# Three-block transformer kernel: the two MLPs' up products with chained weight and input sums, and a new order where each MLP begins

## The chip, the cores and the metric

One core of a Trainium2 chip runs the whole program, one launch. The metric is the time of that launch on the device in microseconds (us), smaller is better. Most of the program is float32 matrix products done on TensorE (PE) as three products of split operands: every operand is cut into a rounded high part (written by ScalarE, ACT) and the remainder, the low part (written by VectorE, DVE, for inputs and by GpSimd, POOL, for weights), and high x high, high x low and low x high are accumulated. SyncE (SP) issues all DMA transfers.

## What is computed

Three blocks follow one another on a sequence of 1024 tokens with 1024 channels: a convolution and a gated recurrence with a mixer, then a block with chunked attention, and then one with an mLSTM. The second and the third block end in an MLP, and the change is in these two (here MLP 2 and MLP 3):

```
hdn = jnp.square(jax.nn.relu(hdn))                       # hdn = rms_norm(x) @ w_up, 1024 x 4096
x = x + jnp.einsum('bsf,fd->bsd', hdn, w_down[l])        # second block
x = layer_norm_3(ALPHA * x + squared_relu_mlp(x, w_ff1[l], w_ff2[l]), ln2_g[l], ln2_b[l])   # third block
```

## The kernel before

Activations stand transposed: 128 channels on the partitions, tokens along the row, so that X is eight tiles of 128x1024. An MLP has 32 tiles of 128 hidden channels. The program treats them in two ways.

**First ups.** The first four tiles (u = 0 to 3) are plain products. The tokens come in two halves (hf 0 and 1, 512 tokens), so there are eight half products, here called h0 to h7. `gemm_half` (L701) is one: eight k tiles, three matmuls of 512 columns each, 24 matmuls. Its weights are one slab of 128x1024: SP fetches it into raw (two places), ACT copies it to wh (L1513, place i % 2), POOL writes wl in two halves (L3662). ACT's split of slab i waits until slab i-2 has been used, since wh has two places. Before the change h0 to h7 use eight slabs, base+0 to base+7: the four weights are loaded and split once for each token half. After each half product ACT evacuates with relu (L2044), DVE squares it (L3041), and SP stores it.

**Fast ups.** The other 28 tiles are 14 pairs. A pair's 2x2 block product (hidden 2, inputs 2x512 channels, tokens 2x512) is done with seven products instead of eight (`fast_mlp`, L1206): 98 products of 12 matmuls, in three groups of four (high x high, high x low, low x high; L1226). The weights of a product are 128x512 in a ring of four places; ACT makes the high part (`w_high`, L2068, runs at L2081) once the product four before is done, POOL the low part (L3679). Of the seven weights of a pair two are blocks of the matrix as it is, and five are sums that DVE makes (`w_add`, L3057, runs at L3071). The inputs are seven as well: two are plain, five are sums of X blocks, made once per MLP: for each of four k tiles a sum by DVE (L3051), a high part by ACT (L2050) and a low part by DVE (L3054). The seven results go to eight PSUM banks in turn; DVE combines them (`hidden`, L3083, adds at L3089), then relu and square in one (L3121, L3130), then five sums that the down products need, and SP stores all (`keep_pair`). A bank is free for the product eight later when its last reader is done (`up_free`, L572).

**Fast downs.** 7 passes of 14 products (L1245), again 12 matmuls each. Weights and hidden tiles come in by DMA; ACT makes the high part of the hidden tile (L2086), DVE the low part (`act_low`, L3073, runs at L3075). DVE's turn n of its loop also makes the weight sum for product n+5, and its in-order queue puts `act_low` of m+3 behind that sum. SP reloads X from DRAM (B<-keep_x) for the later additions.

The order on each engine is the order in which the functions are written. Nothing is scheduled by a planner.

Of the kernel before, what the change touches and what calls it, by code (L numbers as in the profile page):

```python
# [19 lines left out]
KT = 8  # L20
META = 16
# [37 lines left out]
GATES3, POOL3, OUT3, MLP3 = 154, 175, 179, 191  # L59
NSLAB = 206  # L60


def twice(a, b):
# [5 lines left out]
WEIGHTS = [*range(92), *twice(92, 96), *twice(96, 100), *range(100, 122), *twice(122, 126), *twice(126, 130),  # L69
           *twice(130, 134), *twice(134, 138), *range(138, 159), *twice(159, 163), *twice(163, 167), 167,  # L70
           *twice(168, 171)]
# [4 lines left out]
def down_at(base, j, hf=0):  # L76
    return base + 8 + j + hf * (4 - HALVED[base])
# [11 lines left out]

PAIRS = 14  # L90
NUP, NFAST = 7 * PAIRS, 14 * PAIRS
UP_ORDER = (2, 4, 5, 3, 1, 7, 6)
# [11 lines left out]
TAKEN = {4: "21", 3: "12", 1: "22+", 7: "11++", 6: "22++"}  # L104
# [3 lines left out]
def fast_product(n):  # L108
    return UP_ORDER[n % 7] if n < NUP else DOWN_ORDER[(n - NUP) // PAIRS]


SUMMED = [n for n in range(NFAST) if fast_product(n) in W_SUM]
# [161 lines left out]
def program(nc, A, tables, draft):  # L274
# [159 lines left out]
    def spent(i):  # L434
        return c.gemm(i, 1 if i in DOWN else 0)
# [41 lines left out]
    def up_half(u, hf):  # L477
        n = (4 * hf + u) % 6
        return side_of(ub[:, n // 2, :], n % 2)
# [68 lines left out]
    def act_slot(z, m):  # L548
        return IN[2][z][:, m % 4, :]
# [29 lines left out]
    def slab_behind(i):  # L579
        return next((m for m in (MLP2, MLP3) if i in (m + 8, m + 9)), None)  # L580
# [3730 lines left out]
```

## Time and profile before

| | us |
|---|---|
| median of 3 runs (3541.1 to 3544.37) | 3543.8 |
| the profiled execution | 3541.67 |
| its span | 3540.4 |
| TensorE busy, of the span | 3437.9 (97%) |
| VectorE / GpSimd / ScalarE busy | 2406.9 / 1414.0 / 1323.4 |
| granted TensorE clock, mean | 0.99 |

MLP 2's first ups, fast ups and fast downs lie at about 1754 to 1809, 1811 to 2093 and 2093 to 2369 us of the span, MLP 3's at about 2833 to 2896, 2897 to 3181 and 3181 to 3458. TensorE hardly ever waits, so what matters are the few gaps in its stream: their sum, who ends each, and the stretches in which its granted clock is half.

### The profile page before, as it was taken

The numbers are of one execution on the slowest core, as the hardware profiler recorded it, in microseconds if no ns is written. First come the engines' busy times: TensorE is split into PE (matmuls) and PEld (weight loads), VectorE is DVE, ScalarE is ACT, GpSimd is POOL, SyncE is SP. The second block draws the span as 40 slices with busy tenths as digits, with TensorE's granted clock in tenths as the row PEclk, the third lists the DMA queues.
The fourth block names the chain that finished last, engine by engine and source line by source line (L and its number), as shares of the span: only waits on it lengthen the run. The fifth ranks groups of instructions, "written<-read, shape, count | busy, mean of one in ns | idle before, by whom it ended". The sixth has DMA issues, their size and how long they took to land.

```text
span 3540.4 us, 46507 instructions
## 1 busy us (share of the span) xinstructions
PE 3437.9 (97%) x17822; PEld 2839.0 (80%) x17822; DVE 2406.9 (68%) x3137; ACT 1323.4 (37%) x1950; POOL 1414.0 (40%) x916
## 2 busy tenths in 40 slices
PE   8999999999999999999979999999999979999997
PEld 7998888889888887887868877887777758887886
DVE  6677608999653474345488878777566668887786
ACT  5565522222231343443332234444322342234443
POOL 4444422232233451112465545445113455554443
PEclk9999999999999999999999999999999989999998
DMA  3111021111242341111434357544012243447552
GB/s 110 37 31 37 31 90 42 60 60 59 85 143 95 106 153 38 32 32 42 161 110 150 145 213 236 172 122 134 30 36 82 62 135 145 147 159 274 158 172 78
DMA packets 147532, 372.22 MB, mean 105 GB/s; under 512 B 16368, under 2 KB 16624, under 8 KB 147312
## 3 DMA queue, kind: packets, MB, share of 16 engines
q1 hardware_dynamic: 147312, 369.24, 31.1%
q8 instruction: 143, 2.34, 0.3%
q14 instruction: 77, 0.63, 0.1%
HBM read 280.05 MB, written 89.13 MB: 104 GB/s over the span
## 4 chain that ended last, share of the span: by engine, by line
PE 86%; DVE 7%; ACT 2%; DMA 2%; issue 2%; POOL 1%; SPq 0%; DVEq 0%; ACTq 0%
PE psum L669 48%; PE psum L1226 15%; PE psum L1245 14%; PE psum L825 1%; PE psum L1123 1%; PE psum L1090 1%; PE psum L1105 1%; POOL wl L3662 1%; DMA raw<-in_wdn 1%; PE psum L770 1%; POOL wl L3679 0%; DMA B<-keep_x 0%; PE psum L850 0%; PE psum L849 0%; DVE k L3362 0%
## 5 line engine op out<-in xcount | busy, mean ns | idle before, releaser
L3662 POOL TENSOR_TENSOR wl<-raw,wh 128x512 fp32r<-128x512 f32 x412 | 612.4, 1508 | 1316.5 <-ACT wh L1513 1316.5
L669 PE MATMUL psum<-hh,wh 128*128 128x512 f32 (+2 forms) x2864 | 920.7, 389 | 35.5 <-POOL wl L3662 31.2
L669 PE MATMUL psum<-hh,wl 128*128 128x512 f32 (+2 forms) x2864 | 881.5, 376 | 0.0
L669 PE MATMUL psum<-hl,wh 128*128 128x512 f32 (+2 forms) x2864 | 878.0, 375 | 0.0
L669 PEld LDWEIGHTS psum<-hh,wh 128*128 128x128 f32 x2864 | 510.7, 189 | 142.0 <-issue 54.1
L669 PEld LDWEIGHTS psum<-hl,wh 128*128 128x128 f32 x2864 | 526.4, 189 | 93.2
L669 PEld LDWEIGHTS psum<-hh,wl 128*128 128x128 f32 x2864 | 527.2, 189 | 86.5
L3679 POOL TENSOR_TENSOR wl<-wsum,wh 128x512 fp32r<-128x512 f32 x280 | 421.9, 1515 | 391.4 <-ACT wh L2081 391.4
L2081 ACT ACTIVATE wh<-wsum 128x512 fp32r<-128x512 f32 x280 | 176.7, 634 | 484.4 <-PE psum L1245 207.6
L1513 ACT ACTIVATE wh<-raw 128x1024 fp32r<-128x1024 f32 x206 | 217.3, 1055 | 271.7 <-PE psum L669 244.9
L2612 DVE SCALAR_TENSOR_TENSOR psum<-av,vec,psum 128x1024 f32<-128x1024 f32 x232 | 299.2, 1290 | 7.9
L1245 PE MATMUL psum<-hh,wh 128*128 128x512 f32 x784 | 215.2, 396 | 7.8 <-DVE hl L3075 4.0
L1245 PE MATMUL psum<-hl,wh 128*128 128x512 f32 x784 | 212.9, 393 | 0.0
L1245 PE MATMUL psum<-hh,wl 128*128 128x512 f32 x784 | 212.6, 393 | 0.0
L1245 PEld LDWEIGHTS psum<-hh,wh 128*128 128x128 f32 x784 | 147.4, 188 | 43.4 <-issue 4.8
L1245 PEld LDWEIGHTS psum<-hl,wh 128*128 128x128 f32 x784 | 147.7, 188 | 34.2
L1245 PEld LDWEIGHTS psum<-hh,wl 128*128 128x128 f32 x784 | 147.4, 188 | 33.9
L1226 PE MATMUL psum<-hx,wh 128*128 128x512 f32 x672 | 169.5, 394 | 0.0
L3710 POOL TENSOR_TENSOR work<-fb 128x1024 f32<-128x1024 f32 x48 | 115.9, 2423 | 122.4 <-PE psum L825 96.9
L3075 DVE TENSOR_TENSOR hl<-hh_f,hh 128x512 fp32r<-128x512 f32 x100 | 118.1, 1181 | 54.9 <-ACT hh L2086 54.8
L1226 PEld LDWEIGHTS psum<-hx,wh 128*128 128x128 f32 x672 | 126.1, 188 | 29.6
L3075 DVE TENSOR_TENSOR hl<-hl_f,hh 128x512 fp32r<-128x512 f32 x96 | 114.6, 1195 | 46.4 <-ACT hh L2086 46.4
(517 smaller groups left out, 5070.7 us busy)
## 6 DMA issues: line engine op xcount, KB each, us to landing
raw<-in_wts SPq DMA_DIRECT2D x206, 512.0 KB, 3.6
keep_hidden<-B SPq DMA_DIRECT2D x168, 256.0 KB, 2.1
hh_f<-keep_hidden SPq DMA_DIRECT2D x100, 256.0 KB, 2.8
hl_f<-keep_hidden SPq DMA_DIRECT2D x96, 256.0 KB, 2.8
raw<-in_wup SPq DMA_DIRECT2D x28, 512.0 KB, 4.4
rawx<-in_wup SPq DMA_DIRECT2D x28, 512.0 KB, 4.3
raw<-in_wdn SPq DMA_DIRECT2D x56, 256.0 KB, 3.3
rawx<-in_wdn SPq DMA_DIRECT2D x56, 256.0 KB, 3.4
```

Source lines behind the costliest of these rows:

```text
L669: ins = pe.matmul(out, w, x[:, k, c0:c0 + width], start=first and n == only[0], stop=final and n == only[-1])
L770: ins = pe.matmul(x[:, n * 128:(n + 1) * 128], rr[:, slot, a:a + 1].to_broadcast([P, P]), ident, start=True, stop=True)
L825: ins = pe.matmul(x[s0:s0 + 64, a + t0:a + t0 + 64], left[:, b + s0:b + s0 + 64], right[:, b + t0:b + t0 + 64], start=True, stop=True)
L1226: ins = pe.matmul(x, w[:, k * 128:(k + 1) * 128], y[:, k, :], start=(w is a and y is xh and k == 0), stop=(w is b and k == 3))
L1245: ins = pe.matmul(down_bank(base, pi, j), w[:, j * 128:(j + 1) * 128], y, start=(t == 0 and w is a and y is xh), stop=(t == PAIRS - 1 and ...
L1513: se.activation(wh[:, s, :], raw[:, s, :], COPY).then_inc(*c.hi.tick(i))
L2081: se.activation(w_ring(wh, base, n), w_src(base, n), COPY).then_inc(*c.w_hi.tick(base, n))
L2612: ve.scalar_tensor_tensor(Cb[:, m, :] if last else taps, u[:, j:j + T], V("conv_w", 8 * j + m), taps, MUL, ADD).then_inc(*c.cv_dve.tick(*( ...
L3075: ve.tensor_tensor(act_slot(1, m), act_raw(m), fp(act_slot(0, m)), SUB).then_inc(*c.a_lo.tick(base, m))
L3662: gp.tensor_tensor(wl[:, s, a], raw[:, s, a], fp(wh[:, s, a]), SUB).then_inc(*c.lo.tick(i, p))
L3679: gp.tensor_tensor(w_ring(wl, base, n), w_src(base, n), fp(w_ring(wh, base, n)), SUB).then_inc(*c.w_lo.tick(base, n))
L3710: gp.tensor_tensor(lev(lv).rearrange("p (n b) -> p n b", b=2 * hs), bv, bv[:, :, hs - 1:hs].to_broadcast([P, T // (2 * hs), 2 * hs]), SUB) ...
```

## The change

The arithmetic that TensorE does is the same in count: 8 half products and 98 + 98 fast products in each MLP. Around them:

- **Slabs.** The half products run in the order `FIRST_UPS`: tiles 0, 1, 2, 3 on the first token half, then 2, 3, 1, 0 on the second. Tiles 2 and 3 keep their slabs (`HELD`) for both, so an MLP's first ups need six slabs (base+0 to base+5), not eight.
- **Squares.** ACT squares what it evacuated, right behind the relu and waiting for it; DVE no longer does.
- **Fast ups in another form.** Seven products still, but three weights are plain and four are sums, chained (a sum is made of another sum); the inputs are three plain and four sums, chained. The sums to combine the results are seven adds by DVE and one ACT copy a pair, where they were eight and two; each add waits for the one ahead of it.
- **Order.** The products of pairs 0 and 1 are interleaved at the start: (0,1) (1,1) (0,2) (1,2) (0,3) ..., so that the first four need no weight sum and the first five no input sum. Pair 0's weight blocks go to rawx and are fetched before the first ups' last slabs. DVE's input sums have explicit waits for POOL's low parts (`lo(base + 4, 1)`, `lo(base + 5, 1)`, `w_lo(base, 1)`).
- **Up to down.** DVE's last hidden sums are spread over the first six down products, SP stores them between the down loads, and X comes back in halves from down product 12 on, not in whole tiles from 6 on. The first down weights wait for up product 94 (fourth from last), because the cache lies on another input.
- **MLP 3.** The offsets that ACT adds to X (`offset`) are done in halves, the first halves between the relus.

```diff
-UP_ORDER = (2, 4, 5, 3, 1, 7, 6)
+FIRST_UPS = ((0, 0, 0), (1, 1, 0), (2, 2, 0), (3, 3, 0), (2, 2, 1), (3, 3, 1), (4, 1, 1), (5, 0, 1))
+HELD = (2, 3)
+UP_ORDER = (1, 3, 2, 7, 6, 5, 4)
+UPS = ((0, 1), (1, 1), (0, 2), (1, 2), (0, 3), (0, 7), (0, 6), (0, 5), (0, 4), (1, 3), (1, 7), (1, 6), (1, 5), (1, 4),
+       *((j, p) for j in range(2, PAIRS) for p in UP_ORDER))
+UP_ALONE = {1: (0, 0), 2: (0, 1), 4: (1, 1)}
+UP_SUM = {5: ((1, 0), ADD, (1, 1)), 6: (5, SUB, (0, 0)), 3: ((0, 1), SUB, 6), 7: ((0, 0), SUB, (1, 0))}
+UP_IN = {7: ((1, 1), SUB, (0, 1)), 6: (7, ADD, (0, 0)), 5: ((0, 1), SUB, (0, 0)), 4: ((1, 0), SUB, 6)}
+SUM_TURN = {**{5: (1, (5,)), 6: (1, (6, 3)), 7: (1, (7,))},
+            **{7 * j + z: (j + 1, ps) for j in range(1, PAIRS - 1) for z, ps in ((3, (5,)), (4, (6, 3)), (5, (7,)))}}
-TAKEN = {4: "21", 3: "12", 1: "22+", 7: "11++", 6: "22++"}
+TAKEN = {2: "11", 6: "u1", 5: "u3", 7: "u2", 3: "12", 4: "21"}
...
+        def relu_half(base, q):
+            i, u, hf = FIRST_UPS[q]
+            e = int(hf and i in HELD)
+            se.wait_ge(*c.gemm(base + i, e))
...
+            x = up_half(q)
+            se.activation(x, pairs.of(base + i, e)[:, hf, :], ACT.Relu).then_inc(*c.ev.tick("up", base, u, hf))
+            se.wait_ge(*c.ev("up", base, u, hf))
+            se.activation(x, x, SQUARE).then_inc(*c.ev.tick("squared", base, u, hf))
...
+            in_highs(base, 7)
+            for q in range(4, 8):
+                if q < 6:
+                    se.wait_ge(*c.gemm(base + FIRST_UPS[q][0], 1))
+                    split(base + q)
+                relu_half(base, q)
+                if q < 6:
+                    in_highs(base, (6, 5)[q - 4])
...
         def hidden(base, n):
...
+            if p == 2:
...
+                add(h[0, 0], h[1, 0], at[2], "11")
+            elif p == 6:
+                add(h[1, 0], h[1, 0], at[6], "u1")
+            elif p == 5:
+                add(h[0, 1], h[1, 0], at[5], "u3")
...
+                add(h[1, 1], h[0, 1], at[7], "22")
+                add(h[1, 0], h[1, 0], at[7], "u2")
+                add(h[0, 1], h[0, 1], at[3], "12")
+                row_done(base, j, 0)
             else:
+                add(h[1, 0], h[1, 0], at[4], "21")
+                if j < PAIRS - 1:
+                    row_done(base, j, 1)
...
         def fast_mlp(base):
-            for u in range(4):
-                squared(base, u, 0)
-            for u, p in enumerate((4, 1, 7)):
-                in_sums(base, p)
-                squared(base, u, 1)
...
+            in_sums(base, 7)
+            in_sums(base, 6)
+            in_lows(base, 7)
+            ve.wait_ge(*c.lo(base + 4, 1))
+            in_sums(base, 5)
+            in_lows(base, 5)
+            for p in UP_SUM:
+                up_weights(base, 0, p)
+            ve.wait_ge(*c.lo(base + 5, 1))
+            ve.wait_ge(*c.gemm(base + 5, 0))
+            in_sums(base, 4)
+            in_lows(base, 6)
+            ve.wait_ge(*c.w_lo(base, 1))
+            in_lows(base, 4)
...
             if p == 3:
-                sp.wait_ge(*c.fast(base, NUP - 6 if t < 8 else NUP - 5))
+                sp.wait_ge(*c.fast(base, NUP - 4 if t < 8 else NUP - 1))
...
-            for m in range(6):
-                down_step(base, m)
-            keep_pair(base, PAIRS - 1)
+            last = {5: (2,), 6: (5,), 7: (6,), 8: (3,), 9: (1,), 10: (4,), 11: (7,)}
```

**Where MLP 2's first ups end, on ACT.** ub<-psum is the relu of a half product, wh<-raw 128x1024 the split of a slab, hx and hh the high parts of input sums, wh 128x512 that of a fast product's weight. Before:

```order
L1513 ACTIVATE wh<-raw 128x1024 [waits product_done,weight_in0]
L2044 ACTIVATE ub<-psum 128x512 [waits product_done]
L2050 ACTIVATE hx<-hx_f 128x512 [waits input_sum] x4
L1513 ACTIVATE wh<-raw 128x1024 [waits product_done,weight_in1]
L2044 ACTIVATE ub<-psum 128x512 [waits store2,product_done]
L2050 ACTIVATE hx<-hx_f 128x512 [waits input_sum] x4
L2044 ACTIVATE ub<-psum 128x512 [waits store3,product_done]
L2081 ACTIVATE wh<-wsum 128x512 [waits product_done,weight_sum]
L2081 ACTIVATE wh<-raw 128x512 [waits product_done,block1,block0]
L2050 ACTIVATE hh<-hl_f 128x512 [waits input_sum] x4
```

Now (L2068 is the square):

```order
L1532 ACTIVATE wh<-raw 128x1024 [waits product_done,weight_in1]
L2066 ACTIVATE ub<-psum 128x512 [waits product_done]
L2068 ACTIVATE ub<-ub 128x512 [waits evacuated_act]
L2073 ACTIVATE hx<-hx_f 128x512 [waits input_sum] x4
L2066 ACTIVATE ub<-psum 128x512 [waits store2,product_done]
L2068 ACTIVATE ub<-ub 128x512 [waits evacuated_act]
L2066 ACTIVATE ub<-psum 128x512 [waits store3,product_done]
L2068 ACTIVATE ub<-ub 128x512 [waits evacuated_act]
L2108 ACTIVATE wh<-rawx 128x512 [waits product_done,block0]
L2108 ACTIVATE wh<-raw 128x512 [waits product_done,block2]
L2108 ACTIVATE wh<-rawx 128x512 [waits product_done,block0]
```

The square stands between the last relu and the first product's weight, which is a plain block and no sum, and no input sums stand between the first four weights.

**The same place on DVE.** hx_f and hl_f are input sums, hx and hl their low parts, wsum a weight sum. Before:

```order
L3041 TENSOR_TENSOR ub<-ub 128x512 [waits evacuated_act]
L3051 TENSOR_TENSOR hx_f<-B 128x512 x4
L3054 TENSOR_TENSOR hx<-hx_f,hx 128x512 [waits input_sum_hi] x4
L3041 TENSOR_TENSOR ub<-ub 128x512 [waits evacuated_act]
L3051 TENSOR_TENSOR hx_f<-B 128x512 x4
L3054 TENSOR_TENSOR hx<-hx_f,hx 128x512 [waits input_sum_hi] x4
L3041 TENSOR_TENSOR ub<-ub 128x512 [waits evacuated_act]
L3071 TENSOR_TENSOR wsum<-raw 128x512 [waits block1,block0]
L3041 TENSOR_TENSOR ub<-ub 128x512 [waits evacuated_act]
L3071 TENSOR_TENSOR wsum<-raw 128x512 [waits block1,block0] x2
L3051 TENSOR_TENSOR hl_f<-B 128x512 x4
```

Now:

```order
L3067 TENSOR_TENSOR hx_f<-B 128x512 [waits normed] x4
L3067 TENSOR_TENSOR hx_f<-hx_f,B 128x512 [waits normed,input_sum] x4
L3073 TENSOR_TENSOR hx<-hx_f,hx 128x512 [waits input_sum_hi] x4
L3067 TENSOR_TENSOR hx_f<-B 128x512 [waits normed,weight_lo]
L3067 TENSOR_TENSOR hx_f<-B 128x512 [waits normed] x3
L3073 TENSOR_TENSOR hx<-hx_f,hx 128x512 [waits input_sum_hi] x4
L3088 TENSOR_TENSOR wsum<-rawx 128x512 [waits block1,block0]
L3088 TENSOR_TENSOR wsum<-wsum,rawx 128x512 [waits weight_sum]
L3088 TENSOR_TENSOR wsum<-rawx,wsum 128x512 [waits weight_sum]
L3088 TENSOR_TENSOR wsum<-rawx 128x512
L3067 TENSOR_TENSOR hl_f<-B,hx_f 128x512 [waits normed,input_sum,product_done,weight_lo]
```

The four first sums stand ahead of the rest, the squares are gone, and there are waits for weight_lo (POOL's part of slabs base+4 and base+5) and for product_done, the end of h7.

**Where MLP 2's ups turn into downs, on DVE.** The adds read PSUM, the 128x1024 instruction is relu and square of a row, hl<-hh_f,hh is the low part of a down product's hidden tile. Before:

```order
L3089 TENSOR_TENSOR B<-psum,B 128x512 [waits fast_copied]
L3089 TENSOR_TENSOR B<-psum,B 128x512 [waits fast_products]
L3089 TENSOR_TENSOR B<-psum,B 128x512 [waits fast_dve]
L3089 TENSOR_TENSOR B<-psum,B 128x512
L3075 TENSOR_TENSOR hl<-hh_f,hh 128x512 [waits hidden_hi]
L3089 TENSOR_TENSOR B<-B,psum 128x512 [waits fast_dve,fast_products]
L3089 TENSOR_TENSOR B<-B,psum 128x512 [waits fast_dve]
L3075 TENSOR_TENSOR hl<-hh_f,hh 128x512 [waits hidden_hi]
L3089 TENSOR_TENSOR B<-B,psum 128x512 [waits fast_dve,fast_products]
L3121 SCALAR_TENSOR_TENSOR B<-B 128x1024 [waits fast_dve]
L3089 TENSOR_TENSOR B<-B 128x512 [waits hidden_out6,fast_dve]
L3075 TENSOR_TENSOR hl<-hh_f,hh 128x512 [waits hidden_hi]
```

Now:

```order
L3103 TENSOR_TENSOR hl<-hh_f,hh 128x512 [waits hidden_hi]
L3142 TENSOR_TENSOR B<-B,psum 128x512 [waits fast_products]
L3103 TENSOR_TENSOR hl<-hh_f,hh 128x512 [waits hidden_hi,fast_dve]
L3142 TENSOR_TENSOR B<-B,psum 128x512 [waits fast_products]
L3142 TENSOR_TENSOR B<-B,psum 128x512 [waits hidden_out6,fast_dve]
L3142 TENSOR_TENSOR B<-B,psum 128x512 [waits fast_dve] x2
L3113 SCALAR_TENSOR_TENSOR B<-B 128x1024 [waits fast_dve]
L3103 TENSOR_TENSOR hl<-hh_f,hh 128x512 [waits hidden_hi,fast_dve]
L3142 TENSOR_TENSOR B<-B,psum 128x512 [waits fast_products]
L3103 TENSOR_TENSOR hl<-hh_f,hh 128x512 [waits hidden_hi,fast_dve]
L3113 SCALAR_TENSOR_TENSOR B<-B 128x1024
```

Up product 92's bank, the first that a down product writes, is given free by the last add of the group that stands behind product 96 (the row with x2); before, it was given free by the adds behind product 94.

## Rows read from the trace of the kernel before

**Rows 1.** The page, busy time of an engine.

```profile
PE 3437.9 (97%) x17822; PEld 2839.0 (80%) x17822; DVE 2406.9 (68%) x3137; ACT 1323.4 (37%) x1950; POOL 1414.0 (40%) x916
```

**Rows 2.** Waits of PE, whole span: us in total, times, longest.

```profile
PE psum L669 <- POOL wl L3662: 31.2, 8, 11.5
PE psum L1226 <- POOL wl L3679: 12.5, 2, 6.2
PE psum L1226 <- ACT wh L2081: 5.2, 4, 1.3
PE psum L1245 <- DVE hl L3075: 4.0, 2, 2.0
PE psum L1245 <- ACT wh L2081: 3.8, 2, 1.9
```

**Rows 3.** Windows: length, busy and count of PE, PEld, DVE, ACT, POOL, clock, DMA.

```profile
1776.00:1836.00 60.00, 42.05 (x164) 32.46 (x163) 46.59 (x61) 23.92 (x39) 37.70 (x17) 0.89 0.35 113
1900.00:2000.00 100.00, 100.00 (x433) 80.92 (x432) 89.05 (x103) 28.02 (x47) 53.58 (x37) 1.00 0.41 149
2816.00:2836.00 20.00, 15.63 (x66) 12.43 (x64) 17.03 (x22) 9.48 (x14) 10.26 (x8) 0.91 0.18 54
2857.00:2923.00 66.00, 43.70 (x163) 33.50 (x162) 43.05 (x61) 28.78 (x45) 38.28 (x18) 0.84 0.49 167
2093.00:2135.00 42.00, 38.10 (x164) 30.45 (x163) 23.94 (x23) 15.97 (x27) 19.44 (x14) 1.00 0.89 333
3180.00:3227.00 47.00, 43.08 (x179) 34.33 (x178) 28.76 (x29) 18.40 (x31) 20.15 (x16) 0.96 0.91 343
```

**Rows 4.** Windows of a few us behind gaps of PE.

```profile
1798.60:1805.40 6.80, 3.37 (x8) 2.72 (x9) 2.17 (x4) 0.00 (x0) 4.51 (x2) 0.50 0.21 36
3218.60:3222.00 3.40, 3.40 (x8) 2.67 (x9) 3.30 (x4) 1.51 (x3) 2.11 (x2) 0.51 1.05 396
```

**Rows 5.** Timeline of ACT: start, duration, instruction, idle time before; MLP 2's slab base+5.

```profile
1780.26 1.06 ACT L1513 ACTIVATE wh<-raw 128x1024 fp32r<-128x1024 f32 x1 [3.67 <-DMA raw<-in_wts]
```

**Rows 6.** Timeline of POOL, MLP 2's first ups and first fast products.

```profile
1781.41 3.37 POOL L3662 TENSOR_TENSOR wl<-raw,wh 128x512 fp32r<-128x512 f32 x2 [2.43 <-ACT wh L1513]
...
1794.03 9.09 POOL L3662 TENSOR_TENSOR wl<-raw,wh 128x512 fp32r<-128x512 f32 x2 [5.25 <-ACT wh L1513]
...
1817.82 8.29 POOL L3679 TENSOR_TENSOR wl<-wsum,wh 128x512 fp32r<-128x512 f32 x1 [4.21 <-ACT wh L2081]
```

**Rows 7.** Timeline of DVE, one run of input sums in MLP 2's first ups.

```profile
1795.27 2.48 DVE L3051 TENSOR_TENSOR hx_f<-B 128x512 f32<-128x512 f32 x4
```

**Rows 8.** Timeline of ACT: last relu, first weight; a dependent pair; MLP 3's offsets.

```profile
1809.43 0.60 ACT L2044 ACTIVATE ub<-psum 128x512 f32<-128x512 f32 x1 [11.01 <-PE psum L669]
1809.92 0.62 ACT L2081 ACTIVATE wh<-wsum 128x512 fp32r<-128x512 f32 x1
...
2825.80 0.71 ACT L2316 ACTIVATE B<-B,vec 128x512 f32<-128x512 f32 x1
2826.53 0.63 ACT L2318 ACTIVATE hh<-B 128x512 fp32r<-128x512 f32 x1
...
2863.50 5.29 ACT L2328 ACTIVATE B<-B,vec 128x1024 f32<-128x1024 f32 x5
```

**Rows 9.** Timelines: ACT's first down weight; DVE's adds in a pair, an act_low.

```profile
2086.08 0.63 ACT L2081 ACTIVATE wh<-hx_f 128x512 fp32r<-128x512 f32 x1 [1.60 <-DMA hx_f<-in_wdn]
...
1928.56 2.61 DVE L3089 TENSOR_TENSOR B<-psum,B 128x512 f32<-128x512 f32 x4 [0.58 <-ACT B L2104]
...
2094.60 1.78 DVE L3075 TENSOR_TENSOR hl<-hh_f,hh 128x512 fp32r<-128x512 f32 x1
```

**Rows 10.** DMA issues (KB each, median us to landing); DVE's wait, 2120 to 2135.

```profile
hx_f<-in_wdn SPq DMA_DIRECT2D x28, 256.0 KB, 3.3
B<-keep_x SPq DMA_DIRECT2D x16, 512.0 KB, 8.2
...
DVE wsum L3071 <- DMA raw<-in_wdn: 5.6, 1, 5.6
```

More of the change, by code:

```diff
@@ L1200, in first_ups @@
         def first_ups(base, ver):
-            for hf in range(2):
-                for u in range(4):
-                    gemm_half(base + 4 * hf + u, hf, c.ev("up", base, u, hf), ver if u == 0 else None)
-                side.drain()
+            for q, (i, u, hf) in enumerate(FIRST_UPS):
+                gemm_half(base + i, hf, c.ev("up", base, u, hf), ver if q % 4 == 0 else None, int(hf and i in HELD))
+                if q % 4 == 3:
+                    side.drain()
         def fast_mlp(base):
@@ L2124, in fast_mlp @@
                     first_high(base, m - 5 * PAIRS - 4)
-            split(base + 9)
+            split(base + 7)
         split(OUT2 + 3)
@@ L2356, in scalar @@
         half_root("v1", 1)
[L2358 removed]
+        first_ups(MLP3, last_high, offset)
         fast_mlp(MLP3)
@@ L3055, in in_sums, with up_weights @@
             ins.then_inc(*c.in_lo.tick(base, p))
+        def up_weights(base, j, p):
+            n, (a, op, b) = UP_AT[j, p], UP_SUM[p]
+            if p == 5:
+                for z in range(2):
+                    ve.wait_ge(*c.block("up", base, j, z))
+            if j:
+                ve.wait_ge(*c.w_lo(base, UP_AT[j - 1, p]))
+            xs = []
+            for mk in (a, b):
+                if mk in UP_SUM:
+                    ve.wait_ge(*c.w_sum(base, UP_AT[j, mk]))
+                xs.append(up_sum(mk) if mk in UP_SUM else w_block(base, n, mk))
+            ve.tensor_tensor(up_sum(p), *xs, op).then_inc(*c.w_sum.tick(base, n))
         def w_add(base, n):
@@ new lines, in sum_of, with hidden_sums @@
+        def sum_of(base, j, q):
+            a, op, b = IN_SUM[q]
+            if j == 0 and q == 6 and base == MLP3:
+                for k in range(KT):
+                    ve.wait_ge(*c.stored("xm3", k))
+            if j > 1:
+                ve.wait_ge(*c.kept(base, q, j - 2))
+            ve.tensor_tensor(hid_sum(j, q), hid_block(j, a), hid_block(j, b), op).then_inc(*c.post.tick(q, base, j))
+        def hidden_sums(base, j, step):
+            for q in {0: (6, 1), 1: (3,), 2: (4,), 3: (7,)}.get(step, ()):
+                sum_of(base, j, q)
@@ L3091, in sum_of, with add @@
-            def sum_of(q):
-                a, op, b = IN_SUM[q]
-                if j == 0 and q == 6 and base == MLP3:
+            def add(out, a, b, key):
+                ve.tensor_tensor(out, a, b, ADD).then_inc(*c.post.tick(key, base, j))
+                ve.wait_ge(*c.post(key, base, j))
+            if p not in (2, 6, 5, 4):
+                return
+            ve.wait_ge(*c.fast(base, n))
+            if p == 2:
+                ve.wait_ge(*c.copied(base, UP_AT[j, 1]))
+                if j > 1:
+                    ve.wait_ge(*c.kept(base, 2, j - 2))
+                elif j and base == MLP3:
@@ L3675, in fast_mlp @@
         def fast_mlp(base):
-            split(base + 7)
+            split(base + 5)
             for n in range(NFAST):
@@ L3697, in half_lows @@
                 half_low(ver, 5, hf, src(5, hf))
-                split(first + 4 * hf + 4)
+                if not hf or ver not in ("ff2", "ff3"):
+                    split(first + 4 * hf + 4)
                 half_low(ver, 7, hf, src(7, hf))
```

324 lines of the change are left out of this document (144 added, 180 removed).

## The prediction

> **What bounds the kernel now.** I read the page's busy shares first: TensorE (PE) is busy for 97% of the span, DVE for 68% [rows 1]. So only two things can be gained: gaps in PE's stream and stretches at the lower clock. The waits of PE come next [rows 2]: five groups belong to the MLPs' seams and sum to 31.2 + 12.5 + 5.2 + 4.0 + 3.8 = 56.7 us. A wait says nothing of the clock, so I sized the seams with windows [rows 3]. In the steady ups 433 matmuls take 100.00 us, PE busy throughout: 0.231 us each, 2.77 us a fast product of 12, 5.54 us a half product of 24. What a window is longer than its count times 0.231 is lost, gap or clock. MLP 2's beginning (1776 to 1836): 60 - 164 x 0.231 = 22.1. MLP 3's (2857 to 2923): 66 - 163 x 0.231 = 28.3. Where ups turn into downs: 42 - 164 x 0.231 = 4.1 and 47 - 179 x 0.231 = 5.7. Together 60.2 us. Another window of MLP 3 (2816 to 2836) loses 20 - 66 x 0.231 = 4.8; it lies before its half product h0, and the change doesn't reach it.
>
> Part of the loss is clock. After a gap the granted clock falls to 0.50 (1.2 of 2.4 GHz) for some 6.8 us: 8 matmuls in 3.40 us instead of 14.7, 1.6 us lost, and a longer gap's window shows the same 0.50 with idle in it [rows 4]. Both beginnings have two such stretches each (mean clock 0.89 and 0.84 [rows 3]), the second turn a short one (0.96).
>
> Who ends the gaps at a beginning? ACT splits slab base+5 late, having waited 3.67 us for the DMA [rows 5]. POOL's low part of slab base+7 took 9.09 us for two halves, and that of fast product 2's weight 8.29 for one, where two halves elsewhere take 3.37 [rows 6]. In these two cases POOL was issued into a run of DVE instructions with two SBUF inputs (input sums, four in 2.48 us [rows 7]), and did not finish until the run was over, some 12 instructions later. And products 0 and 2 wait 1.3 us each for `w_high` [rows 2], which stands behind the last relu [rows 8]. At the turn, one gap of 2.0 us waits for `act_low`, in a DVE queue full of the last hidden sums (one `act_low` took 1.78 [rows 9]); another, of 1.9 us some 30 us on, begins with a `w_add` that waits 5.6 us for its block, while X returns in tiles that take 8.2 us to land [rows 10].
>
> **First ups: slabs and squares.** h4 and h5 now use slabs whose split is long done, so the gap before h5 goes. Slab base+4 is split when h4 has ended, and used by h6, one half product (5.54 us) later; the split takes 1.06 [rows 5] and POOL 3.37 even where it is contended [rows 6]: 4.4, hidden by h5. Slab base+5 has the same behind h5. Its fetch stands behind pair 0's blocks in SP's queue, but its place in raw is free once base+3 is split, behind h1: four half products less 4.4, some 17 us ahead of need. If that cover failed, the 3.67 us would be back. The explicit DVE waits for POOL keep the long runs of input sums behind these low parts: the 7.4 us gap ahead of h7 goes. DVE's own delay from these waits matters only for the input sums, and the first needs one at product 5, 14 us into the fast ups. Eight squares (0.6 each) leave DVE for ACT, which is 37% busy.
>
> **First fast product.** Now: last relu, square, first `w_high`. The square waits for the relu, and two dependent ACT instructions start 0.73 apart (2825.80 and 2826.53), where relu and weight now start 0.49 apart (1809.43 and 1809.92) [rows 8]. PE's wait grows from 1.3 by one more square, 0.65 to 0.73: 1.3 + 0.66 and 0.15 of pipeline restart = 2.1. Products 1 to 3 need plain blocks only, their `w_high` is done 0.62 apart against 2.77 a product: the 1.3 of product 2 goes. The low part of product 0 (POOL, used by its last four matmuls, 1.85 us in) is issued when DVE starts `in_sums` 4 and `in_lows` 6, which wait for h7: POOL comes a few instructions into that run. I take the near row, the contended halves (3.37 / 2, 0.4 more than a free one of 1.3): 0.2. If it isn't let in before the run of 8 ends (8 x 0.62 = 5.0 us), product 0 stops about 2.3. Product 2's 6.2 us go, because `in_lows` 4 waits for `w_lo` and no run as long as the old one is ahead of it. MLP 2's beginning keeps 2.1 + 0.2 = **2.3 of 22.1**.
>
> At this place a rule of the Trainium skill speaks (SBUF — State Buffer, "Who interferes with whom"): a DVE instruction with two SBUF inputs and a GpSimd one that reads SBUF exclude each other, and whoever issues first holds the port for its whole instruction. By that rule alone POOL would wait for the rest of one DVE instruction, at most 0.68, and product 0 wouldn't stop: the sum as it stands. The trace differs [rows 6]; by its long cases there would be 2.3 more in each MLP, the first rival.
>
> **MLP 3's beginning.** The same 2.3, and the offsets. Five whole ones took 5.29, 1.06 each [rows 8]. Now the late halves of five (5 x 0.6 = 3.0) and four high parts of input sums (2.5) stand ahead of slab base+4's split on ACT, behind h3's relu and square (1.35): done 6.8 us into h4, 1.3 after its end. With 4.4 for the split h6 is late by 1.3 + 4.4 - 5.54 = 0.2, up to 1.45 if ACT waits in between (the sums come from DVE), and 0 if POOL has its halves uncontended (2.6). I take 0.7. It keeps **3.0 of 28.3**.
>
> **Steady ups.** Per pair there is one weight sum less, one add less and one ACT copy less. PE never waited there (100.00 busy of 100.00, with DVE at 89.05 [rows 3]), so this brings nothing. It can cost: each add now waits for the one ahead, and the four of product 5's group free their banks one by one. Four adds took 2.61 [rows 9]; with the waits 2.9. The last ("12") frees the bank that the product eight later, 5.5 us further on, writes: hidden. Zero. SP's queue has the same number of blocks and stores a pair, and POOL the same low parts.
>
> **Ups to downs.** The first down weight is fetched once product 94 is done, three products (8.3 us) ahead of the end, landing 3.3 later [rows 10], at -5.0 counted from the end of the ups. ACT splits weight and hidden tile (0.63 each [rows 9]), `act_low` 0.7: -3.0. On DVE's queue follow the add "u1", the second `act_low` (about -1.1), then the four adds, 2.7: +1.6. `act_low` can be contended (1.78 instead of 0.7), once or twice: +2.3 to +3.2. This last add frees the bank of up product 92, which down product 0 writes. So PE stops for 2.35 us (1.6 to 3.2) at product 0, in place of the 2.0. Behind it DVE has less in its queue than before. The second stall goes: X is asked for from down product 12, so the block for `w_add` isn't among 512 KB transfers, and with it goes the 1.6 of clock in MLP 3. The two turns keep **4.7 of 9.8**.
>
> **Sum.** Gaps left: 2.3 + 3.0 + 4.7 = 10.0. A gap of about 2 dropped the clock in one turn and not in the other [rows 3], so of the four left I count one drop, 1.7: 11.7. The gain is 60.2 - 11.7 = 48.5; the profiled execution, 3541.67, comes to 3493.2. The median is 2.1 above it: **3495**. With nothing contended (turns 1.6 each, MLP 3's slab in time, no clock drop) 3488; with everything at its upper end, 3507.
>
> **Rivals.** *POOL is starved in new places.* Product 0 stops 2.3 more in each MLP, MLP 3's slab takes the full 1.45 (+0.75), and each of these gaps of 4 drops the clock (3 x 1.7): 4.6 + 0.8 + 5.1 = 10.5 more, about 3505. For it: the 8.29 and 9.09 of [rows 6]. Against: both were issued early in a run of 12 and more, and the new run is 8. 15%.
>
> *The beginnings wait for something else.* The slabs' fetch and ACT's chain (relu, square, sums, split) take the place of POOL, and of the 50.4 us there only half goes: 3495 + 23 = 3518. For it: the 3.67 us of DMA wait [rows 5], and in MLP 3 five offsets on the same queue. Against: 17 us of lead for the fetch, ACT 37% busy. 8%.
>
> *Slower: the steady ups pay for the chained adds.* There are 28 pairs; to eat 48.5 us each would have to lose 1.73, so the last add would be 5.5 + 1.7 = 7.2 us later than I counted. From a delay of 5.5 on PE would stop in each pair. For it: DVE at 89% [rows 3] and POOL's contention, which stretches some of its instructions to twice. Against: DVE loses two instructions a pair, and four adds take 2.61. 3%, some 3560.
>
> **How the numbers follow.** Forecast as it stands 72% (3488 to 3507), first rival 15%, second 8%, third 3%; 2% that the new form's count or order costs a few us and gains nothing. The range 3484 to 3510 holds the forecast and the first rival; its lower end has 4 us for parts counted too dear (the old turns' other losses, MLP 3's window of 4.8). About 0.2% (7 us) is what a measurement can tell from no change: even 3518 is 0.7% faster. Faster 0.95, same 0.02, slower 0.03.
>
> **What would show it.** In the profile after: no wait of PE for the slabs' wl above 1.5 us; one wait of about 2 for `w_high` ahead of product 0 in each MLP, none ahead of product 2; POOL's first fast low parts at 1.3 to 2, not 8; clock above 0.95 in both beginnings; one wait of 1.6 to 3.2 at down product 0, ended by DVE's adds, no second one; the steady ups at 433 matmuls in 100 us. Waits of PE for DVE in the steady ups would prove the last rival, a POOL instruction of 5 or more at product 0 the first, a split that waits for a DMA the second.

## The result: 3482.5 us, 12.5 us below the forecast, and a fifth of the gain in another place

| | before | changed |
|---|---|---|
| median of 4 runs (us) | 3543.7 | 3482.47 (3480.15 to 3485.08) |
| span of the profiled execution | 3540.4 | 3481.2 |
| TensorE busy | 97% | 99% |

The ratio is 0.983, 95% interval 0.981 to 0.985: a gain of 61 us where 48.5 were forecast. The time lies 1.5 us below the range's lower end of 3484, so the range missed it.

The page of the changed kernel, busy time of an engine, against [rows 1]: TensorE (PE) is busy 8 us less for the same 17,822 matmuls (its clock is low for less of the span, 0.993 on average where it was 0.990), GpSimd (POOL) 38 us less.

```profile
PE 3429.6 (99%) x17822; PEld 2839.3 (82%) x17822; DVE 2389.7 (69%) x3049; ACT 1309.7 (38%) x1931; POOL 1376.2 (40%) x908
```

The waits of PE, whole span (us in total, times, longest), against [rows 2]:

```profile
PE psum L690 <- POOL wl L3710: 8.6, 3, 4.4
...
PE psum L1266 <- DVE B L3142: 5.1, 2, 2.7
PE psum L1247 <- ACT wh L2108: 3.9, 2, 2.0
```

The slabs' 31.2 us are 8.6, and none of these is left in the two places that the change reaches (4.4 of it is the gap ahead of MLP 3's h0, which the prediction left alone). The 8.6 were there before as well: of the 31.2 only 9.1 and 13.5 us lay in the two beginnings. The 12.5 us for fast weights' low parts are gone. The turn has one wait per MLP, now for an add.

Windows that hold the same matmuls as stages of before (columns as in [rows 3]): the two beginnings, the two turns, then three stretches with low clock behind the waits.

```profile
1766.90:1840.20 73.30, 71.34 (x301) 57.40 (x300) 60.05 (x68) 31.59 (x55) 36.79 (x26) 0.98 0.26 87
2819.50:2882.30 62.80, 60.83 (x262) 48.69 (x261) 57.28 (x62) 35.40 (x60) 33.67 (x22) 1.00 0.44 159
2063.10:2136.90 73.80, 71.08 (x301) 57.33 (x301) 52.22 (x57) 28.85 (x50) 34.60 (x25) 0.98 0.87 313
3112.10:3176.40 64.30, 61.95 (x262) 49.88 (x261) 43.49 (x47) 24.92 (x43) 29.16 (x22) 0.97 0.89 313
1799.00:1806.00 7.00, 6.87 (x23) 5.52 (x24) 7.00 (x6) 3.74 (x8) 6.94 (x5) 0.76 0.10 37
2075.00:2082.00 7.00, 5.25 (x17) 4.27 (x18) 5.88 (x8) 1.20 (x3) 1.27 (x2) 0.76 0.57 203
3122.40:3129.00 6.60, 4.58 (x14) 3.68 (x15) 6.43 (x8) 1.26 (x2) 1.54 (x2) 0.74 0.64 231
```

By the prediction's measure (length less count times 0.231) they still lose 3.8, 2.3, 4.3 and 3.8 us, 14.2 together, where before lost 60.2: the seams gave 46.0 us.

The two programs have the same 17,822 matmuls, so I cut both traces at the same ones and compared the lengths. The table holds starts of matmul n to matmul m, in us, worked out from the two traces:

| stage (matmuls) | before | changed | gain |
|---|---|---|---|
| up to MLP 2's first ups (0 to 10,340) | 1759.9 | 1758.8 | 1.1 |
| MLP 2's beginning (to 10,640) | 91.8 | 73.4 | 18.5 |
| MLP 2's steady ups (to 11,600) | 222.8 | 222.9 | -0.1 |
| MLP 2's turn (to 11,900) | 73.8 | 73.8 | 0.0 |
| downs (to 12,900) | 231.7 | 231.7 | 0.0 |
| **third block up to MLP 3 (to 15,050)** | **464.5** | **450.9** | **13.7** |
| MLP 3's beginning (to 15,310) | 88.9 | 62.8 | 26.1 |
| MLP 3's steady ups (to 16,300) | 229.7 | 229.9 | -0.1 |
| MLP 3's turn (to 16,560) | 66.2 | 64.2 | 1.9 |
| downs (to 17,550) | 228.9 | 228.9 | 0.0 |
| end | 63.7 | 65.5 | -1.7 |

The MLPs' stages gave 46.3 us against 48.5 forecast, nearly all of it at the two beginnings: MLP 2's turn gained nothing and MLP 3's 1.9. What comes on top is one row for which the prediction has no term: 13.7 us in the third block, between the MLPs. (The end takes 1.7 us back; the granted clock is 0.85 there, where it was 0.88.)

Its waits show it. Before, PE's waits from 2388 to 2852 us:

```profile
PE psum L669 <- POOL wl L3662: 7.1, 2, 4.4
PE psum L1371 <- DVE h L3327: 4.2, 7, 1.5
PE psum L1317 <- ACT v L2216: 3.6, 1, 3.6
PE psum L1399 <- DVE B L3346: 1.6, 1, 1.6
PE psum L1360 <- DVE den L3302: 1.2, 3, 0.4
```

Of the changed kernel, from 2368 to 2820 us:

```profile
PE psum L690 <- POOL wl L3710: 7.0, 2, 4.4
PE psum L1336 <- DVE eT L3317: 0.7, 1, 0.7
PE psum L1400 <- DVE h L3387: 0.3, 2, 0.2
PE psum L690 <- DVE hl L2430: 0.2, 1, 0.2
```

10.6 us of waits at small products of the mLSTM became 1.0. The code of the mLSTM is the same in both. What differs is an edit at the end of the MLP's matmul function (`fast_mlp` of TensorE). It is in the diff, but in none of the parts by which I went through the change, and the excerpt ahead of the prediction leaves it out:

```diff
-            aux.only(*(psum[:, f[z], :] for z in (4, 5, 6)))
-            aux.freed = [fold_done(base, 6, j) for j in range(3)]
-            head.only(psum[:, f[7], :])
-            head.freed = [fold_done(base, 6, 3)]
+            aux.only(*(psum[:, f[z], :] for z in (4, 5, 6, 7)))
+            aux.freed = [fold_done(base, 6, j) for j in range(4)]
```

`aux` is the ring of PSUM banks for TensorE's side work (transposes, the mLSTM's small products), which is threaded between the big matmuls; `head` is a ring that nothing behind MLP 2 takes from. Behind an MLP the side work had three banks, and one lay idle; now it has four.

### The profile page after: what moved, and what is told of

Its sections match the earlier page's. It is cut to its first block, busy times and chain, and to the rows that moved or that the text cites. A ratio compares the mean times of both kernels' runs of the same rounds, so it can differ in the third digit from the quotient of the medians.

```text
span 3481.2 us, 46333 instructions
## 1 busy us (share of the span) xinstructions
PE 3429.6 (99%) x17822; PEld 2839.3 (82%) x17822; DVE 2389.7 (69%) x3049; ACT 1309.7 (38%) x1931; POOL 1376.2 (40%) x908
## 2 busy tenths in 40 slices
DMA packets 149258, 370.10 MB, mean 106 GB/s; under 512 B 16560, under 2 KB 16816, under 8 KB 149040
## 4 chain that ended last, share of the span: by engine, by line
PE 90%; DVE 6%; ACT 1%; issue 1%; DMA 0%; POOL 0%; SPq 0%; DVEq 0%; ACTq 0%
PE psum L690 49%; PE psum L1266 16%; PE psum L1247 15%; PE psum L846 1%; PE psum L1144 1%; PE psum L1111 1%; PE psum L1126 1%; PE psum L791 1%; PE psum L871 0%; PE psum L870 0%; DVE hl L2430 0%; DVE k L3410 0%; PE psum L862 0%; DVE h L3387 0%; DVE h L3375 0%
## 5 line engine op out<-in xcount | busy, mean ns | idle before, releaser
L3710 POOL TENSOR_TENSOR wl<-raw,wh 128x512 fp32r<-128x512 f32 x404 | 584.9, 1468 | 1307.7 <-ACT wh L1532 1307.7
L3727 POOL TENSOR_TENSOR wl<-wsum,wh 128x512 fp32r<-128x512 f32 x252 | 366.3, 1455 | 345.9 <-ACT wh L2108 345.8
L2108 ACT ACTIVATE wh<-wsum 128x512 fp32r<-128x512 f32 x252 | 159.9, 635 | 448.7 <-PE psum L1266 218.2
```

Source lines behind the costliest of these rows:

```text
L2108: se.activation(w_ring(wh, base, n), w_src(base, n), COPY).then_inc(*c.w_hi.tick(base, n))
L3710: gp.tensor_tensor(wl[:, s, a], raw[:, s, a], fp(wh[:, s, a]), SUB).then_inc(*c.lo.tick(i, p))
L3727: gp.tensor_tensor(w_ring(wl, base, n), w_src(base, n), fp(w_ring(wh, base, n)), SUB).then_inc(*c.w_lo.tick(base, n))
```

## The experiments

The lengths named below are those of the table's stages, by the same cuts. `three_banks`, `before_four_banks`, `both_first` and `all_moved` were timed four or five times, the other six once. The changed kernel's own four times lie 4.9 us apart, so a single time within a few us of another shows little; the stage lengths carry the argument.

**Is it the fourth bank?** Two kernels that differ by that edit alone, each from its own side. `three_banks` is the changed kernel with the four lines, and one that waited for the points of both rings, back as they were:

```diff
-                    for point in aux.freed:
+                    for point in (*aux.freed, *head.freed):
...
-            aux.only(*(psum[:, f[z], :] for z in (4, 5, 6, 7)))
-            aux.freed = [fold_done(base, 6, j) for j in range(4)]
+            aux.only(*(psum[:, f[z], :] for z in (4, 5, 6)))
+            aux.freed = [fold_done(base, 6, j) for j in range(3)]
+            head.only(psum[:, f[7], :])
+            head.freed = [fold_done(base, 6, 3)]
```

> The changed kernel with one edit undone: behind each MLP the ring of PSUM banks for TensorE's side work has three banks again, and the fourth lies idle in a ring of its own. Theory A (the ring's fourth bank is what made the third block's mLSTM shorter, 450.9 us from the end of MLP 2's downs to MLP 3's half products against 464.5 before): that stretch takes 462 to 466 us again, the waits of PE's line in the mLSTM for DVE h and ACT v come back (some 10 us in all), and the time is 3492 to 3499 us. Theory B (it was the schedule that the new MLP 2 hands over, or chance between two executions): the stretch stays at 450 to 453 and the time at 3480 to 3485.

Measured: 3495.7 us (3493.3 to 3496.4), and the third block's stage is back at 464.4. PE's waits from 2369 to 2833 us are those of before, to a few tenths:

```profile
PE psum L1392 <- DVE h L3377: 3.8, 7, 1.5
PE psum L1338 <- ACT v L2240: 3.6, 1, 3.6
PE psum L1420 <- DVE B L3396: 1.6, 1, 1.6
PE psum L1381 <- DVE den L3352: 1.2, 3, 0.4
```

`before_four_banks` is the kernel before with the same edit the other way.

> The kernel before with only that edit: four banks in the ring of the side work behind each MLP, none in the other. Theory A: the stretch of the third block between MLP 2's downs and MLP 3's half products takes 449 to 453 us instead of 464.5, both MLPs' seams are unchanged, and the time is 3528 to 3533 us. Theory B: the stretch and the time (3541 to 3545) stay.

Measured: 3528.85 us against 3544.8 of before on the same chip, ratio 0.996 (0.994 to 0.997); the stage takes 450.95, and both beginnings are as before (92.3 and 88.8). So theory A holds from both sides, for 13.5 and 13.6 us, and theory B falls.

`two_banks` takes a second bank away from the changed kernel's ring, to see whether the ring's length or one unlucky position counts.

```diff
...
-            aux.only(*(psum[:, f[z], :] for z in (4, 5, 6, 7)))
-            aux.freed = [fold_done(base, 6, j) for j in range(4)]
+            aux.only(*(psum[:, f[z], :] for z in (4, 5)))
+            aux.freed = [fold_done(base, 6, j) for j in range(2)]
+            head.only(psum[:, f[6], :], psum[:, f[7], :])
+            head.freed = [fold_done(base, 6, 2), fold_done(base, 6, 3)]
```

> The changed kernel with only two PSUM banks in the side work's ring behind each MLP. If the ring's length sets how far TensorE's side work in the mLSTM can run ahead of DVE and ACT, each bank less costs more than the one before: the stretch from MLP 2's downs to MLP 3's half products, 450.9 us with four banks and 464.4 with three, takes 480 us or more, all in waits for DVE and ACT, and the seams of the MLPs stay. If the third run's 13.5 us were a matter of one unlucky position in the ring, two banks cost about as much as three (460 to 468).

Measured: 481.8 us for the stage, 3513.45 in all. Four, three and two banks give 450.9, 464.4 and 481.8. The waits of PE from 2368 to 2851 us:

```profile
PE psum L1392 <- DVE h L3377: 10.0, 5, 2.7
...
PE psum L1381 <- DVE den L3352: 6.3, 3, 2.1
PE psum L1352 <- DVE eT L3319: 2.5, 1, 2.5
...
```

PE's waits at the side products are 20.2 us here, 10.2 with three banks and 1.0 with four. They are not all of the stage's loss: the mean granted clock over the stage is 0.97 with two banks, 0.99 with three and four.

One of the waits shows the mechanism closely. In the timeline of before, PE starts to spread the gate rows (line 1317), which needs two banks of the ring, 3.59 us late. By the code the second of them is, in a ring of three, the bank that holds the first half of the transposed `v`, and the wait is for ACT's copy out of it; ACT had a table load, an evacuation and a weight split to do first:

```profile
2487.18 1.21 PE L1317 MATMUL psum<-row,cst 4*128 4x256 f32 x8 [3.59 <-ACT v L2216]
...
2483.28 1.28 ACT L2244 ACT_TABLE_LOAD   x1
2484.57 1.02 ACT L2244 ACTIVATE o<-psum 128x1024 f32<-128x1024 f32 x1
2485.49 1.05 ACT L1513 ACTIVATE wh<-raw 128x1024 fp32r<-128x1024 f32 x1
2486.44 1.08 ACT L2216 ACTIVATE v<-psum 128x512 f32<-128x512 f32 x2
```

In the changed kernel ACT does the same at the same distance, but PE's product starts 2.1 us ahead of the copy of `v`, in a bank that the copy doesn't hold:

```profile
2464.94 1.13 PE L1336 MATMUL psum<-row,cst 4*128 4x256 f32 x8 [0.74 <-DVE eT L3317]
...
2467.05 1.08 ACT L2238 ACTIVATE v<-psum 128x512 f32<-128x512 f32 x2
```

The waits make 9.6 of the 13.7 us; of the rest a part is clock. Behind that gap of 3.59 a 40 us window of before has a granted clock of 0.96:

```profile
2480.00:2520.00 40.00, 36.01 (x195) 29.26 (x195) 20.66 (x49) 13.47 (x14) 5.03 (x4) 0.96 0.08 27
```

The window of the changed kernel at the same place has 1.00:

```profile
2459.00:2499.00 40.00, 39.26 (x221) 32.25 (x220) 25.46 (x58) 15.72 (x17) 5.08 (x4) 1.00 0.08 27
```

**Was POOL starved by DVE's runs, and do the new waits prevent it?** Two halves of one step of the prediction. `before_pool_waits` adds waits to the kernel before:

```diff
             for u, p in enumerate((4, 1, 7)):
+                if u:
+                    ve.wait_ge(*c.lo(base + 5 + u, 1))
                 in_sums(base, p)
...
             in_sums(base, 3)
+            ve.wait_ge(*c.w_lo(base, 2))
             in_sums(base, 6)
```

> The kernel before, with DVE waiting for POOL's part of slabs base+6 and base+7 ahead of its second and third group of input sums, and of product 2's weight ahead of the last. If starvation by DVE's runs made the 7.4 and 6.2 us gaps, POOL's two instructions of 8 us are gone there, and MLP 2's beginning (91.8 us) falls by 8 to 16 us, MLP 3's (88.9) by 8 to 20, less 0 to 3 each for sums that now come late. If the gaps were late slabs (DMA, ACT), they stay within 2 us.

Measured: 3520.9 us, the beginnings 80.9 and 79.7 instead of 91.8 and 88.9, so 10.9 and 9.2 less. POOL's two instructions are short again (3.69 for both halves of slab base+7, 2.30 for product 2's low part, against 9.09 and 8.29 of [rows 6]):

```profile
1791.57 3.69 POOL L3665 TENSOR_TENSOR wl<-raw,wh 128x512 fp32r<-128x512 f32 x2 [5.25 <-ACT wh L1513]
...
1809.95 2.30 POOL L3682 TENSOR_TENSOR wl<-wsum,wh 128x512 fp32r<-128x512 f32 x1 [4.22 <-ACT wh L2081]
```

So the starvation was real and its reading from [rows 6] and [rows 7] holds, and it was half of MLP 2's loss and a third of MLP 3's. (Some of the sums then came late: PE has a wait of 3.5 us for a weight's high part in MLP 3's beginning, where its waits for high parts were 1.3 each.)

`no_pool_waits` takes the three waits out of the changed kernel:

```diff
-            ve.wait_ge(*c.lo(base + 4, 1))
             in_sums(base, 5)
...
-            ve.wait_ge(*c.lo(base + 5, 1))
             ve.wait_ge(*c.gemm(base + 5, 0))
...
-            ve.wait_ge(*c.w_lo(base, 1))
             in_lows(base, 4)
```

> The changed kernel without DVE's three waits for POOL (slab base+4, slab base+5, the weight of product 1); its input sums then run as soon as their operands are there. If the waits are what keeps POOL from being starved by a run of DVE instructions with two SBUF inputs, one POOL instruction of 5 us or more is back in at least one of the MLPs' beginnings, with a wait of PE for it of 2 us or more and 3 to 12 us more in total. If the shorter list of slabs and sums alone removed the stalls, no POOL instruction there is over 4 us and both beginnings stay at 73 and 63 us by the same count of matmuls.

Measured: 3483.2 us, the beginnings 71.8 and 62.7. POOL's longest there is 4.55 for two halves; PE waits for neither:

```profile
1780.89 4.55 POOL L3707 TENSOR_TENSOR wl<-raw,wh 128x512 fp32r<-128x512 f32 x2 [7.45 <-ACT wh L1532]
...
1786.45 2.55 POOL L3707 TENSOR_TENSOR wl<-raw,wh 128x512 fp32r<-128x512 f32 x2 [1.01 <-ACT wh L1532]
...
1798.21 1.80 POOL L3724 TENSOR_TENSOR wl<-rawx,wh 128x512 fp32r<-128x512 f32 x1 [9.20 <-ACT wh L2108]
```

The second expectation is the right one: the waits aren't what prevents the starvation. The rest of the change does, and which part of it isn't shown. It isn't the squares' move to ACT, since with the squares on DVE again (`squares_dve`, below) no POOL instruction of MLP 2's beginning is long either (4.78 us for two halves, 1.35 for product 0's low part). The shorter slab list and the new order of the sums are left; they weren't tried apart.

**What makes the 2.0 us ahead of product 0?** `squares_dve` has the squares on DVE again (one behind each place where DVE had it before, SP's stores waiting for DVE):

```diff
-            se.wait_ge(*c.ev("up", base, u, hf))
-            se.activation(x, x, SQUARE).then_inc(*c.ev.tick("squared", base, u, hf))
...
+            ve.wait_ge(*c.ev("up", base, u, hf))
+            ve.tensor_tensor(x, x, x, MUL).then_inc(*c.post.tick(("sq", u, hf), base, 0))
```

> The changed kernel with the squares of the half products on DVE again. By the prediction's step the square is 0.65 of the 2.0 us that PE waits for the first fast product's weight: the wait falls to about 1.3 in both MLPs, and the beginnings (73.4 and 62.8 us by count) get 0.5 to 2.5 us shorter. If DVE's queue is the tighter one there, an input sum comes late instead, PE waits for in_lows at product 5 or later, and the beginnings get 1 to 5 us longer.

Measured: the wait is 1.3 in both MLPs, as the step said, but only MLP 2's beginning gets shorter (71.1, without the stretch of low clock); MLP 3's is 63.7, with a new wait of 1.7 for a relu. So the square is 0.7 of the 2.0 us. The one time is 3485.7, but 2.8 us of it are a longer third block (453.6), with the same waits of PE there and the clock low for longer, so it doesn't say which engine is the better place for the squares.

`weights_first` keeps the squares on ACT and lets the first two weights go ahead of them:

```diff
+                if q == 7:
+                    w_high(base, 0)
+                    w_high(base, 1)
                 relu_half(base, q)
...
-                w_high(base, n)
+                if n > 1:
+                    w_high(base, n)
```

> The changed kernel, with ACT's high parts of the weights of fast products 0 and 1 ahead of the last half product's relu and square instead of behind them (their place is free once the half product before has ended, 5.5 us earlier). If the 2.0 us wait of PE ahead of product 0 is the length of that ACT chain, both waits go and with each the stretch at half clock behind it: 4 to 8 us less over both MLPs' beginnings. If something else comes last there (POOL's low part, the PSUM banks), a wait of 1 to 2 us stays under another name and the gain is under 2 us.

Measured: 3476.9 us. No gap of PE is left in either beginning; they take 69.6 and 60.6, 301 and 262 times 0.231 and no more, so the ACT chain was all of it. (MLP 2's turn, which the edit doesn't touch, took 75.4 instead of 73.8, with a wait of 3.0 instead of 2.7.)

```profile
1766.00:1835.60 69.60, 69.60 (x301) 56.34 (x300) 60.82 (x68) 31.68 (x55) 36.27 (x26) 1.00 0.27 91
2817.00:2878.00 61.00, 60.98 (x263) 49.12 (x262) 56.21 (x61) 33.21 (x57) 35.18 (x21) 1.00 0.43 160
```

**What makes the stall at the turn?** The changed kernel's timelines of DVE and PE there (the four adds, and the first down product):

```profile
2070.76 0.69 DVE L3103 TENSOR_TENSOR hl<-hh_f,hh 128x512 fp32r<-128x512 f32 x1 [6.46 <-ACT hh L2113]
2071.37 0.68 DVE L3142 TENSOR_TENSOR B<-B,psum 128x512 f32<-128x512 f32 x1
2072.77 1.08 DVE L3103 TENSOR_TENSOR hl<-hh_f,hh 128x512 fp32r<-128x512 f32 x1 [0.71 <-ACT hh L2113]
2073.76 2.84 DVE L3142 TENSOR_TENSOR B<-B,psum 128x512 f32<-128x512 f32 x4
...
2076.75 2.04 PE L1266 MATMUL psum<-hh,wh 128*128 128x512 f32 x4 [2.72 <-DVE B L3142]
```

DVE idles 6.46 us for the first hidden tile, with the adds behind `act_low` in its queue. `adds_first` turns them round:

```diff
-                add(h[1, 0], h[1, 0], at[7], "u2")
                 add(h[0, 1], h[0, 1], at[3], "12")
+                add(h[1, 0], h[1, 0], at[7], "u2")
...
-                if m >= -3 and m + 3 < NFAST - NUP:
+                if m >= -1 and m + 3 < NFAST - NUP:
                     act_low(base, m + 3)
...
                     hidden(base, n)
+                    if m in (-3, -2):
+                        act_low(base, m + 3)
```

> The changed kernel, with DVE's adds of up products 95 and 96 ahead of the first two low parts of hidden tiles, and the add that frees up product 92's bank one place earlier. If the stall of 2.4 to 2.7 us where ups turn into downs is that add's place in DVE's queue, it falls to 0 to 0.5 us in both MLPs, the half clock behind it goes, and each turn gains 2 to 4 us. If not the bank but the first low part or the weight's DMA is the limit, a wait of 1 to 2 us appears at down product 0 or 1 instead.

Measured: 3472.95 us; the turns take 71.4 and 61.4 instead of 73.8 and 64.2. That is 5.2 of the 9.5 us by which this one time lies below the changed kernel's; the others lie in stages that the edit doesn't touch. The waits fell less than expected: in MLP 2 1.1 us for the add and 0.3 for `act_low` are left (below), in MLP 3 0.8 for a weight's high part:

```profile
2072.70 1.36 PE L1266 MATMUL psum<-hh,wh 128*128 128x512 f32 x4 [1.08 <-DVE B L3142]
2076.15 1.16 PE L1266 MATMUL psum<-hh,wh 128*128 128x512 f32 x4 [0.26 <-DVE hl L3103]
```

`both_first` is the sum of the last two edits.

> The changed kernel with both rearrangements (ACT's first two weights ahead of the last relu; DVE's adds ahead of the first low parts at the turn). If they act in different places they add up: 3.8 and 2.2 us less at the two beginnings, 2.3 and 2.9 at the two turns, 3470 to 3474 us, faster than the changed kernel by 0.2% to 0.35%. If the clock only moves its low stretch elsewhere, 3475 to 3480.

Measured: 3469.27 us (3467.6 to 3470.5), ratio to before 0.979 (0.978 to 0.981); the changed kernel stands at 0.983 (0.981 to 0.985). The beginnings take 69.6 and 60.5, the turns 70.9 and 61.4: 3.8, 2.2, 2.9 and 2.9 us less than in the changed kernel, so the two edits add up. The time is 0.7 us below the expected 3470 to 3474. At the turns a wait for `act_low` is left, 1.2 and 0.7 us.

`all_moved` adds one exchange in POOL's queue, ahead of MLP 3's first half product:

```diff
                 half_low(ver, 3, hf, src(3, hf))
+                if ver == "ff3" and not hf:
+                    split(first + 4)
                 half_low(ver, 5, hf, src(5, hf))
```

> As both_first, and in the third block POOL's low part of the slab of MLP 3's first half products ahead of one low part of an input tile, since PE waits 4.4 us for that slab in every kernel so far. If that order is the cause, the 4.4 us wait falls to under 2, and the time is 1.5 to 5 us below both_first's. If the slab was late by ACT, the wait and the time stay.

Measured: 3470.8 us (3469.6 to 3471.8), no better. The wait ahead of h0 fell from 4.4 to 0.4 us, but 7 us behind it PE waits for a DVE instruction that it didn't wait for in `both_first`, so the expected 1.5 to 5 us didn't come (of the waits of the whole span):

```profile
PE psum L690 <- POOL wl L3716: 4.7, 3, 2.7
...
PE psum L781 <- DVE t L3486: 2.6, 1, 2.6
```

The 4.4 us were POOL's order, as supposed, and the gain went into a new wait; the stage got 0.7 us shorter (450.1 against 450.8).

## Why the prediction was right or wrong

- **Where the kernel was bound.** Near on the four seams together: 60.2 us lost there, 46.0 given back, 48.5 forecast. The two beginnings carry that (45.1 forecast without the clock, 44.6 measured); the turns fell short, as said below. The prediction also puts all five groups of [rows 2], 56.7 us, at the seams; 8.6 of the slabs' 31.2 lay elsewhere and stayed. Its sum goes by the windows, so that slip cost nothing. Wrong in what it left out. The same view of PE's waits that gave the five groups of [rows 2] also had 10.6 us at the mLSTM's side products; the sentence that only gaps and clock can be gained was followed by a choice of the gaps that the change seemed to be about.
- **The step that failed** is the list of the change's parts. It went by the themes of the edit (slabs, squares, sums, order, turn, offsets), and the four lines on the rings of PSUM banks belong to none. So the sum has terms for the seams alone and puts the third block at nothing, without a reason. With these lines most of the term could have been had from the trace of before: side products that wait 10.6 us for readers of a bank in a ring of three, and a fourth bank. It measured 13.5 to 13.7 us by three pairs of kernels, and carries all of the miss of 12.5: 3495 less 13.7 is 3481.
- **First ups and their slabs.** Right: no wait for a slab is left in either MLP's first ups. The explicit waits of DVE, which the step credits with the 7.4 us gap, aren't needed (`no_pool_waits`).
- **First fast product.** Wait ahead of product 0 forecast 1.96, measured 2.0 twice; none ahead of product 2; POOL's low part of product 0 took 1.8, not starved. MLP 2 keeps 3.8: 2.1 (the wait and the restart) and one drop of the clock.
- **The port rule.** POOL did get in quickly beside DVE's input sums and low parts (1.84 us an instruction; the run was 12 long and not 8, since POOL had done what the wait before the last four asks for), as the Trainium skill's rule of a lock for one instruction would have it (SBUF — State Buffer, "Who interferes with whom"); DVE's four low parts took 6.86 us beside it:

```profile
1799.68 6.86 DVE L3073 TENSOR_TENSOR hx<-hx_f,hx 128x512 fp32r<-128x512 f32 x4
...
1799.06 1.84 POOL L3727 TENSOR_TENSOR wl<-rawx,wh 128x512 fp32r<-128x512 f32 x1 [9.20 <-ACT wh L2108]
```

  But the rule alone doesn't explain the 8.29 us of [rows 6], which `before_pool_waits` took away. Why POOL gets in at one place and not at another stays open.
- **MLP 3's beginning.** Forecast 3.0 kept, 2.3 measured: the offsets delayed nothing. The stall ahead of h0 stayed (4.4), as said.
- **Steady ups.** Zero forecast; 0.1 us longer in each MLP. The chained adds cost nothing and one sum less gained nothing.
- **Turns.** Forecast one stall of 1.6 to 3.2 each, measured 2.72 and 2.35, ended by that add, and the second stall gone: right by mechanism. The term was mis-sized in the clock. I counted one drop for all four gaps; there were three, one at each turn and one at MLP 2's beginning. So the turns kept 4.3 and 3.8, not 2.35 each, and gained 0.0 and 1.9 us where 5.1 together were forecast: in MLP 2 the 1.2 us less of waiting went into a stretch of low clock that the kernel before didn't have there.
- **Rivals.** Starved POOL in new places, a fetch that comes last, and slower steady ups: none happened.
- **The range.** The 3488 for "nothing contended" doesn't follow from its terms: 3495 less 1.5 at the turns, 0.7 for MLP 3's slab, 0.2 twice at product 0 and 1.7 of clock is 3491. Its lower end let 4 us for "parts counted too dear". The miss was not in a price but in a part that wasn't on the list, and no bound of the listed parts covers that.

## What to carry to other kernels

Go through a diff by its lines, not by its themes: each line that changes a pool's size, a ring or who may use a buffer is a term of its own, wherever its users are, and they can be in another stage than the rest of the change. Then set the groups of waits beside the list, those too that no part seems to touch: a small product that waits for a reader of its output bank may ask for one more bank. When the same work is done in both programs, cutting both traces at the same matmuls shows in one table where each microsecond went.

## What the runs showed of the hardware

- Each PSUM bank taken from the ring for side work cost more than the one before it: the stage took 450.9, 464.4 and 481.8 us with four, three and two banks (13.5, then 17.4 more; two banks by a single execution).
- A wait of PE of 2.0 us behind which the clock drops in one kernel leaves it at full speed in another, and at another place of the same kernel (MLP 3's beginning, clock 1.00 in its row above). MLP 2's beginning has the same wait for `w_high` in the changed kernel (granted clock 0.76 in the 7 us behind it, rows above) and in `no_pool_waits`, in the same 7 us:

```profile
1799.00:1806.00 7.00, 7.00 (x32) 5.60 (x32) 7.00 (x5) 4.90 (x10) 7.00 (x5) 1.00 0.02 8
```

MLP 2's beginning is 1.6 us shorter there for it (71.8 against 73.4). Together with waits that differ a little from kernel to kernel (1.9 to 3.2 us at MLP 3's turn) this makes stage lengths that differ by up to 2.5 us between kernels that are alike there (MLP 3's turn 63.9 to 66.3, the end 63.7 to 66.2). What decides whether the clock falls behind a wait of 2.0 us isn't shown.
